# Output projections with their sums of squares accumulated on TensorE, and another order at the start of the up-projection

## The chip, the cores and the metric

The kernel runs on one core of one Trainium2 chip. The core has five engines with a queue each: TensorE (PE, matrix products; PEld is its weight load), VectorE (DVE), ScalarE (ACT), GpSimd (POOL) and SyncE (SP, which issues DMAs here). They run side by side and meet only through semaphores. The metric is the device time of one execution of the whole program in microseconds (us).

## The reference, cut to what matters

Two decoder layers over 1024 prompt and 32 sample tokens, width 1024. What the change touches is, in each layer, the output projection with its norm and residual, and the up-projection of the ConvFFN behind it:

```python
def rms_norm(x, g):
    y = xf * lax.rsqrt(jnp.mean(xf * xf, axis=-1, keepdims=True) + NORM_EPS)
    return (y * g.astype(jnp.float32)).astype(x.dtype)
...
    xp = xp + rms_norm(op, norm_mix_post[i])        # op: the mixer's output @ w_out
    hp = rms_norm(xp, norm_ffn_pre[i])
    fp, cp = conv_ffn(hp, ffn_w_up[i], ffn_conv_w[i], ffn_conv_b[i], ffn_w_down[i], ...)
...
def conv_ffn(h, w_up, conv_w, conv_b, w_down, prev):
    u = h @ w_up
    full = jnp.concatenate([prev.astype(u.dtype), u], axis=1)
    c = conv_b + sum(conv_w[j] * full[:, j:j + T] for j in range(CONV_W))
```

The sample tokens take the same path with their own conv state `prev`.

## The kernel before

Activations lie feature-major in SBUF as [128, 8, 1056] fp32: 8 blocks of 128 features (the keys k), 1056 tokens. The program is a row of stages, each with its own semaphores and an all-engine barrier at its end. Inside a stage the order on each engine is written out by hand; nothing reorders it.

**`stage_out`** (named "aout" in layer 0, "ro" in layer 1) multiplies by the 1024 x 1024 output weights in 12 steps, `STEPS`: 3 chunks c of 352 tokens (`CW`), and in each 4 steps q, every step making output blocks q and q + 4. A step is a Strassen-like scheme of 7 products of 4 matmuls of 176 columns (line L2044; a fp32 matmul stands as two rows in the trace), into banks a, d, b, c, a, cc, d. VectorE forms token mixes t1, t2, t4 (`mix_tokens`) and weight mixes (`mix_weights`), and empties the banks with five additions per step (L2238 to L2254, counted by `evac`); ScalarE copies bank a twice.

Then there are two norms for each chunk. The first: ScalarE squares each finished block (L2144), VectorE adds the squares up in `total` (L2190, `add_squares`, seven additions per chunk, the last ones one step late or, for the last chunk, behind the loop), TensorE sums over partitions with one matmul against ones (`sums`, L2054), ScalarE takes the root (L2107), VectorE the reciprocal (`invert`, L2194), and VectorE scales each key and adds the x of before, which SP fetched from DRAM (`residual`, L2207 and L2199). The second norm, over the new x, gives `K.rstd` for the up-projection: ScalarE squares the 8 keys (`square_again`, L2112) into the used-up source, VectorE folds 8 to 4 to 2 to 1 (`fold`, L2219), TensorE sums (`sums_again`, L2060), ScalarE root (L2116), VectorE reciprocal (`invert_again`, L2223). Chunk c's residual stands in chunk c + 1's steps 1 to 3; that of chunk 2 stands behind the loop. SP stores each finished chunk of x (`keep`, L2028), fetches the third chunk of the old x once chunk 0 is kept, and prefetches the first gate weights of the up-projection (`follow`, L2034).

**`Taps`** brings the conv taps and the conv state (16 rows of 5632) in and turns them on TensorE behind step 1 (L1914, L1916: 44 transposes of 16 x 128), VectorE copies them out of PSUM (L1921, L1922).

**`stage_ffn_up`** first norms x into `hT` on VectorE: for each key two pieces of 512 columns (`scale_half`, L2430) and one of the 32 samples (L2435), the lower four keys first. Then VectorE makes four token mixes of [128, 2112] (t1 L2462, t3 L2467, t2 L2470, t4 L2473) with the four weight mixes s1 to s4 (L2442 to L2449) between them. After that a loop over 22 pairs of blocks runs with 7 products of 8 matmuls each of 264 columns (L2369, order a, d, b, c, a, c, d). The gates of the first products are these lines:

```python
                    pe.wait_ge(first_done, j + 1)          # L2378, first product "a"
                    pe.wait_ge(scaled, 3 * HK)
...
                    pe.wait_ge(evac, ev(j, 0))             # L2383, product "d"; ev(0, 0) is 1
...
            act.wait_ge(zeroed, 2)                         # L2401
            act.sem_inc(first_done, 1)
...
                dve.wait_ge(tmade, 3)                      # L2472, ahead of t4
            dve.tensor_tensor(t4, b21, t2, ALU.subtract).then_inc(tmade, 1)
            for u in range(2):
                dve.memset(ubuf[u][:, 0:2], 0.0).then_inc(zeroed, 1)
            dve.sem_inc(conved, 1)
            dve.sem_inc(evac, 1)                           # L2477
```

## Time and profile before

| | us |
|---|---|
| median of 3 runs | 4861.34 |
| lowest, highest | 4851.31, 4864.03 |
| the profiled execution, its device time | 4863.29 |
| its span in the trace | 4861.7 |
| TensorE busy | 4188.1 (86%) |
| VectorE busy | 2951.7 (61%) |
| ScalarE busy | 1111.3 (23%) |
| GpSimd busy | 318.2 (7%) |

Busy time is the sum over the span; a busy TensorE is a modelled one, since matmuls are pipelined. Its mean granted clock was 0.93 of full speed. The shares are averages over stages with different limits, so the argument rests on timelines of single stages: a timeline lists the instructions of an engine in order of time, merged where they are alike, each with its start and length, and in brackets the idle time ahead of it and what ended it. L-numbers are lines of the kernel, "q" behind an engine's name is its queue.

### The profile page before, as it was taken

The numbers are of one execution on the slowest core, as the hardware profiler recorded it, in microseconds if no ns is written. First come the engines' busy times: TensorE is split into PE (matmuls) and PEld (weight loads), VectorE is DVE, ScalarE is ACT, GpSimd is POOL, SyncE is SP. The second block draws the span as 40 slices with busy tenths as digits, with TensorE's granted clock in tenths as the row PEclk, the third lists the DMA queues.
The fourth block names the chain that finished last, engine by engine and source line by source line (L and its number), as shares of the span: only waits on it lengthen the run. The fifth ranks groups of instructions, "written<-read, shape, count | busy, mean of one in ns | idle before, by whom it ended". The sixth has DMA issues, their size and how long they took to land. (4 is left out here: it accounts for less than half of the span.)

```text
span 4861.7 us, 83795 instructions
## 1 busy us (share of the span) xinstructions
PE 4188.1 (86%) x33219; PEld 3210.0 (66%) x33248; DVE 2951.7 (61%) x4318; ACT 1111.3 (23%) x2118; POOL 318.2 (7%) x443
## 2 busy tenths in 40 slices
PE   7998889877777879999996999678887859999998
PEld 5565335444434768887994655377875758888897
DVE  3799665379942665556465122478885665555465
ACT  1200454344432212222110011132222112222100
POOL 0000000300045000000000000022220000000000
PEclk9999999899978889999997999799998779999999
DMA  3012000299976211111452231422213221111343
GB/s 102 22 35 60 9 1 1 59 320 353 366 230 169 69 47 43 43 43 47 131 147 73 71 112 66 156 63 55 64 38 155 63 72 43 43 40 38 99 143 119
DMA packets 553343, 463.37 MB, mean 95 GB/s; under 512 B 77346, under 2 KB 472138, under 8 KB 548827
## 3 DMA queue, kind: packets, MB, share of 16 engines
q1 hardware_dynamic: 522210, 409.36, 26.8%
q10 hardware_dynamic: 21088, 32.80, 2.0%
q0 software_dynamic: 9728, 16.80, 1.2%
q8 instruction: 222, 3.64, 0.3%
q14 instruction: 95, 0.77, 0.0%
HBM read 397.01 MB, written 61.71 MB: 94 GB/s over the span
## 5 line engine op out<-in xcount | busy, mean ns | idle before, releaser
L313 PE MATMUL proj_acc<-hT,oT 128*128 128x352 f32 x864 | 258.7, 463 | 6.2 <-SPq L287 6.2
L313 PEld LDWEIGHTS proj_acc<-hT,oT 128*128 128x128 f32 x864 | 165.6, 192 | 99.6 <-SPq L287 7.1
L517 DVE TENSOR_SCALAR_CACHE_REDUCE oT<-scores,proj_cand 128x384 bf16<-128x384 f32 (+1 forms) x186 | 164.4, 943 | 1.1
L2416 ACT ACTIVATE fup_c<-fup_c 128x1072 f32<-128x1072 f32 x44 | 48.3, 1098 | 504.6 <-DVEq L2486 504.6
L3424 POOL TENSOR_TENSOR scan_om<-scan_low,scan_level 128x512 f32<-128x512 f32 x80 | 133.1, 1675 | 391.8 <-PE scan_u L3506 294.7
L1227 DVE MAX8 sstick_best<-vtok 32x8 f32<-32x4100 f32 x32 | 141.1, 4408 | 0.0
L1230 DVE MATCH_REPLACE8 vtok<-sstick_best,vtok 32x4100 f32<-32x4100 f32 x32 | 140.8, 4400 | 0.0
L2640 PE MATMUL fdown_acc<-hidden,h 128*128 128x176 f32 x792 | 124.5, 316 | 9.3 <-SPq L2603 9.3
L2640 PE MATMUL fdown_acc<-hidden,oT 128*128 128x176 f32 x792 | 123.8, 315 | 9.4 <-SPq L2603 9.4
L1140 ACT ACTIVATE sstick_kT<-sstick_tp 128x512 f32<-128x512 f32 x248 | 128.3, 597 | 3.6 <-PE sstick_tp L1033 3.5
L2512 DVE TENSOR_TENSOR fup_u<-rstd,fup_acc_c 128x512 f32<-128x512 f32 x44 | 30.3, 689 | 162.3 <-PE fup_acc_c L2369 162.3
L2640 PEld LDWEIGHTS fdown_acc<-hidden,h 128*128 128x128 f32 x792 | 121.4, 193 | 9.7 <-SPq L2603 9.7
L2640 PEld LDWEIGHTS fdown_acc<-hidden,oT 128*128 128x128 f32 x792 | 120.7, 192 | 9.9 <-SPq L2603 9.9
L2485 DVE SCALAR_TENSOR_TENSOR fup_c<-fup_u,taps,fup_c 128x1072 f32<-128x1072 f32 x88 | 117.4, 1335 | 13.4 <-DVE fup_c L2484 5.9
L2484 DVE SCALAR_TENSOR_TENSOR fup_c<-fup_u,taps,fup_c 128x1072 f32<-128x1072 f32 x88 | 117.4, 1335 | 12.2 <-DVE fup_c L2483 4.7
L1804 DVE SCALAR_TENSOR_TENSOR mixed<-xx,vectors,h 128x352 f32<-128x352 f32 (+1 forms) x128 | 69.9, 625 | 68.2 <-PEq L95 68.2
L2369 PE MATMUL fup_acc_a<-oT,w_up_first 128*128 128x264 f32 x352 | 84.7, 395 | 27.6 <-ACTq L2402 27.6
L2369 PE MATMUL fup_acc_a<-h,w_up_first 128*128 128x264 f32 x352 | 83.5, 391 | 27.5 <-ACTq L2402 27.5
L2499 DVE TENSOR_TENSOR fup_u<-rstd,fup_acc_c 128x528 f32<-128x528 f32 x44 | 31.0, 705 | 124.8 <-PE fup_acc_c L2369 124.8
L2413 ACT ACTIVATE fup_u<-fup_acc_a 128x512 f32<-128x512 f32 x44 | 26.3, 599 | 351.8 <-PE fup_acc_a L2369 351.8
L3506 PE MATMUL scan_u<-scan_Tm,scan_om 64*64 64x64 f32 x2560 | 95.3, 233 | 12.4 <-DVE scan_TT L3836 6.4
L3506 PEld LDWEIGHTS scan_u<-scan_Tm,scan_om 64*64 64x64 f32 x2560 | 90.1, 148 | 17.3 <-issue 17.2
(736 smaller groups left out, 9891.8 us busy)
## 6 DMA issues: line engine op xcount, KB each, us to landing
fup_w<-in_ffn_w_up SPq DMA_DIRECT2D x66, 512.0 KB, 4.9
h<-in_ffn_w_down SPq DMA_DIRECT2D x48, 704.0 KB, 4.7
oT<-in_ffn_w_down SPq DMA_DIRECT2D x48, 704.0 KB, 4.7
scores<-in_cache_sb_k SPq DMA_DIRECT2D x128, 256.0 KB, 5.9
qb<-in_cache_sb_k SPq DMA_DIRECT2D x128, 256.0 KB, 6.1
qi<-in_cache_sb_v SPq DMA_DIRECT2D x128, 256.0 KB, 5.9
ka<-in_cache_sb_v SPq DMA_DIRECT2D x128, 256.0 KB, 6.1
w_up_first<-in_ffn_w_up SPq DMA_DIRECT2D x22, 512.0 KB, 3.9
```

The source lines that it names most:

```text
L313: last = pe.matmul(acc[u][0:m, c, 0:CW], w[u][:, k, 0:m], hT[:, k, c * CW:(c + 1) * CW], start=(k == 0), stop=(k == KD - 1))
L517: self.mark(dve.tensor_scalar(self.junk[:, at:at + (CHOOSING[t] + 1) * P], score, at_least, 0.0, ALU.is_ge, ALU.add, accum_out=self.count[ ...
L1140: act.activation(kT[:, p % 2, :, i % 4, (i // 4) * P:(i // 4 + 1) * P], tp[t % 3][:, :].rearrange("p (f n) -> p f n", f=HP), ACT.Copy).the ...
L1227: link(dve.max(best[:, :], score))
L1230: link(dve.match_replace(score, best[:, :], score, LOW))
L1804: dve.scalar_tensor_tensor(out=m[:, k, at], in0=xx[:, k, at], scalar=column[:, k:k + 1], in1=h[:, k, at], op0=ALU.mult, op1=ALU.add).then_ ...
L2369: last = pe.matmul(acc[n][:, g, 0:GW], weights[:, k, :], moving[:, k, g * GW:(g + 1) * GW], start=begin and k == 0, stop=k == HK - 1, skip ...
L2484: link(dve.scalar_tensor_tensor(out=c, in0=ubuf[u][:, 1:1 + CO], scalar=tap[1], in1=c, op0=ALU.mult, op1=ALU.add))
L2485: link(dve.scalar_tensor_tensor(out=c, in0=ubuf[u][:, 2:2 + CO], scalar=tap[2], in1=c, op0=ALU.mult, op1=ALU.add))
L2640: last = pe.matmul(bank[n], weights[:, k, :], moving[:, k, :], start=begin and k == 0, stop=k == DOWN_K - 1, skip_group_check=True)
L3424: pool.tensor_tensor(om[:, heads(g), :], low2[:, heads(g), 0, :], level[:, l, :].unsqueeze(1).to_broadcast(full), ALU.mult).then_inc(om_re ...
L3506: last = pe.matmul(spot(h, c, False), om[half(c), h, :], Tm[half(c), h, :], start=True, stop=True, skip_group_check=True)
```

## The change

Sizes are as before, and the same values are computed, except for the order of additions.

- `Taps`: the state comes in four DMAs as 64 rows of 1408 and is turned by 11 transposes of 64 x 128; two copies put it in place.
- `sums` (first norm) accumulates three matmuls in PSUM: `total` and the two squares of a chunk's last step, which VectorE adds no more (5 additions per chunk). It stands in the next chunk's step 0 instead of 1. `invert` and `residual` move one step ahead likewise.
- Second norm: squares go into the free `before` buffer. Chunk 0 keeps the fold, one step earlier than before; chunks 1 and 2 have none, TensorE accumulates their 8 squares (`sums_of_all`) behind the loop. `square_again`, `root_again` and `invert_again` move with them.
- Chunk 0 is normed in `stage_out` (`normed`) behind the last evacuation, into the place that the up-projection reads.
- SP fetches the third chunk of x after `summed_again` 1, and `follow` now also brings the first value weights.
- `stage_ffn_up`: the two memsets come first, then four keys with 160 columns (`scale_first`, the rest of the first half) and the samples; then the other pieces. The first product waits for 8 scalings instead of 12.
- Buffers only: `raw`, `Z` in the recurrence, and `s4` and `inverse` in the down-projection lie elsewhere.

```diff
     def allocate(self, s):
-        self.state_rows = s.sb("state_rows", [16, 2 * D_FF])
+        self.state_rows = s.sb("state_rows", [64, KF // 2 * P])
...
-        sp.dma_start(self.state_rows[:, :], self.state.rearrange("b w n -> (b w) n")).then_inc(self.loaded, 16)
+        wide = KF // 2 * P
+        for j in range(4):
+            sp.dma_start(self.state_rows[16 * j:16 * j + 16, :], self.state.rearrange("b w n -> (b w) n")[:, j * wide:(j + 1) * wide])\
+              .then_inc(self.loaded, 16)
...
-        for m in range(M):
-            last = pe.transpose(acc[:, m // KF, m % KF * 16:m % KF * 16 + 16], self.state_rows[:, m * P:(m + 1) * P], K.ident[0:16, 0:16])
+        for i in range(KF // 2):
+            last = pe.transpose(acc[:, i // 8, i % 8 * 64:i % 8 * 64 + 64], self.state_rows[:, i * P:(i + 1) * P], K.ident[0:64, 0:64])
...
         def squares(c):
-            return src[:, :, chunk(c)]
+            return before[:, c % 2]
...
             keep(0)
+            sp.wait_ge(summed_again, 1)
             sp.dma_start(before[:, 0], x_before_dram[:, :, chunk(2)]).then_inc(fetched, 16)
...
             def sums(c):
-                pe.wait_ge(totalled, 7 * (c + 1))
+                pe.wait_ge(totalled, 5 * (c + 1))
...
-                pe.matmul(spare[:, 0, 0:CW], K.ones[:, :], total[:, :], start=True, stop=True).then_inc(summed, 1)
...
+                pe.matmul(spare[:, 0, 0:CW], K.ones[:, :], total[:, :], start=True, stop=False)
+                for i in range(2):
+                    pe.wait_ge(squared, 8 * c + 7 + i)
+                    last = pe.matmul(spare[:, 0, 0:CW], K.ones[:, :], square[:, i, :], start=False, stop=i == 1)
+                last.then_inc(summed, 1)
...
+            def sums_of_all(c):
+                if c == 1:
+                    pe.wait_ge(rooted_again, 1)
+                for k in range(KD):
+                    pe.wait_ge(squared_again, KD * c + k + 1)
+                    last = pe.matmul(spare[:, c, 0:CW], K.ones[:, :], squares(c)[:, k, :], start=k == 0, stop=k == KD - 1)
+                last.then_inc(summed_again, 1)
...
-                if c >= 1 and q == 1:
+                if c >= 1 and q == 0:
                     sums(c - 1)
-                if c == 2 and q == 2:
-                    sums_again(0)
+                if c == 2 and q == 1:
+                    sums_folded(0)
...
-            sums_again(1)
             sums(NCH - 1)
-            sums_again(NCH - 1)
+            sums_of_all(1)
+            sums_of_all(2)
...
-                if c >= 1 and q == 1:
+                if c >= 1 and q == 0:
                     root(c - 1)
-                if c == 2 and q == 0:
-                    square_again(0)
-                if c == 2 and q == 2:
+                if c >= 1 and q == 3:
+                    square_again(c - 1)
+                if c == 2 and q == 1:
                     root_again(0)
...
+            def normed(ks):
+                for k in ks:
+                    if k == 0:
+                        dve.wait_ge(inverted_again, 1)
+                        dve.wait_ge(product, 7 * 8)
+                    for low, high, shift in normed_pieces(0):
+                        dve.scalar_tensor_tensor(out=src[:, k, low + shift:high + shift], in0=dst[:, k, low:high], scalar=K.gain[:, k:k + 1],
+                                                 in1=K.rstd[:, low:high], op0=ALU.mult, op1=ALU.mult)
...
-            invert_again(0)
-            add_squares(LAST)
-            fold(1)
+            normed(tuple(range(KD)))
             invert(NCH - 1)
             residual(NCH - 1, tuple(range(KD)))
             invert_again(1)
-            fold(NCH - 1)
             invert_again(NCH - 1)
...
-                    pe.wait_ge(scaled, 3 * HK)
+                    pe.wait_ge(scaled, 2 * HK)
                     multiply("a", gate[:, lower, :], b11, True)
...
+            def scale_first(k):
+                at, low = slice(CW, 2 * GP), CW + GS
...
+            for u in range(2):
+                dve.memset(ubuf[u][:, 0:2], 0.0).then_inc(zeroed, 1)
             for k in range(HK):
-                scale_half(k, 0)
+                scale_first(k)
                 scale_samples(k)
             for k in range(HK):
-                scale_half(k, 1)
+                scale_second(k)
+            dve.wait_ge(scaled, 3 * HK)
             for k in range(HK, KD):
-                scale_half(k, 0)
-                scale_half(k, 1)
+                scale_first(k)
                 scale_samples(k)
+                scale_second(k)
             dve.wait_ge(scaled, 3 * KD)
...
-            for u in range(2):
-                dve.memset(ubuf[u][:, 0:2], 0.0).then_inc(zeroed, 1)
             dve.sem_inc(conved, 1)
             dve.sem_inc(evac, 1)
...
     def follow(self):
-        return [(self.w_up[:, :, :], up_first(self.I.ffn_w_up[self.layer]))]
+        W = self.I.ffn_w_up[self.layer].rearrange("(k p) n -> p k n", p=P)
+        return [(self.w_up[:, :, :], W[:, :, 0:P]), (self.w_up_value[:, :, :], W[:, :, D_FF:D_FF + P])]
```

The code is written by hand in the order in which each engine runs it. VectorE at the end of aout, from the last evacuation to the residual of chunk 2, before:

```order
L2254 TENSOR_TENSOR h<-aout_u,aout_acc_d 128x176
L2207 SCALAR_TENSOR_TENSOR h<-h,aout_gcol,aout_inverse 128x352 x2
L2199 TENSOR_TENSOR h<-h,aout_before 128x352 x2
L2223 RECIPROCAL rstd<-rstd 128x352
L2190 TENSOR_TENSOR aout_total<-aout_total,aout_square 128x352 x2
L2219 TENSOR_TENSOR oT<-oT 128x4x352
L2219 TENSOR_TENSOR oT<-oT 128x2x352
L2219 TENSOR_TENSOR oT<-oT 128x352
L2194 RECIPROCAL aout_inverse<-aout_inverse 128x352
```

and with the change, where the pair L2239 stands eight times:

```order
L2283 TENSOR_TENSOR h<-aout_u,aout_acc_d 128x176
L2239 SCALAR_TENSOR_TENSOR oT<-h,gain,rstd 128x256
L2239 SCALAR_TENSOR_TENSOR oT<-h,gain,rstd 128x96
...
L2214 RECIPROCAL aout_inverse<-aout_inverse 128x352
L2227 SCALAR_TENSOR_TENSOR h<-h,aout_gcol,aout_inverse 128x352 x2
```

What stood between the last evacuation and the reciprocal of chunk 2 has gone into the steps ahead or to TensorE, and the norming of chunk 0 stands there. TensorE behind the last product of aout, before:

```order
L2044 MATMUL aout_acc_d<-oT,aout_mixes 128x176 x4
L2060 MATMUL aout_spare<-oT,ones 128x352
L2054 MATMUL aout_spare<-aout_total,ones 128x352
L2060 MATMUL aout_spare<-oT,ones 128x352
L92 UNCONDITIONAL_BRANCH
```

and with the change:

```order
L2062 MATMUL aout_acc_d<-oT,aout_mixes 128x176 x4
L2072 MATMUL aout_spare<-aout_total,ones 128x352
L2075 MATMUL aout_spare<-aout_square,ones 128x352 x2
L2087 MATMUL aout_spare<-aout_before,ones 128x352 x16
L92 UNCONDITIONAL_BRANCH
```

The sum of chunk 2 (L2072, L2075) no longer stands behind that of the new chunk 1. VectorE in the up-projection of layer 0, before:

```order
L2430 SCALAR_TENSOR_TENSOR oT<-h,gain,rstd 128x2x256
L2435 SCALAR_TENSOR_TENSOR oT<-h,gain,rstd 128x4x8
...
L2462 TENSOR_TENSOR h<-oT 128x2112
...
L2473 TENSOR_TENSOR h<-oT,h 128x2112
L2475 MEMSET fup_u 128x2 x2
L2528 UNCONDITIONAL_BRANCH
```

and with the change:

```order
L2482 MEMSET fup_u 128x2 x2
L2454 SCALAR_TENSOR_TENSOR oT<-h,gain,rstd 128x160
L2465 SCALAR_TENSOR_TENSOR oT<-h,gain,rstd 128x4x8
...
L2460 SCALAR_TENSOR_TENSOR oT<-h,gain,rstd 128x2x256 x4
...
L2506 TENSOR_TENSOR h<-oT,h 128x2112
L2559 UNCONDITIONAL_BRANCH
```

The memsets have moved from behind t4 (L2473, now L2506) to the front; the two increments of semaphores behind t4 have no row here and stand where they stood.

## Rows read from the trace of the kernel before

**Rows 1.** Busy time of each engine in two windows: us, busy us (instructions), PEclk, DMA share, GB/s

```profile
1677.00:1709.00 32.00, 4.27 (x7) 1.68 (x6) 25.74 (x33) 9.17 (x20) 0.00 (x0) 0.56 0.25 90
1709.00:1733.00 24.00, 0.00 (x0) 0.00 (x0) 22.87 (x31) 0.00 (x0) 0.00 (x0) 0.50 0.24 66
```

**Rows 2.** Timeline, TensorE: start us, us, engine line op, shapes, count [idle before <- releaser]

```profile
1733.32 6.46 PE L2369 MATMUL fup_acc_a<-oT,w_up_first 128*128 128x264 f32 x16 [27.62 <-ACTq L2402]
...
1743.18 3.72 PE L2369 MATMUL fup_acc_b<-h 128*128 128x264 f32 x16
...
3974.73 5.34 PE L2369 MATMUL fup_acc_a<-h,w_up_first 128*128 128x264 f32 x16 [27.50 <-ACTq L2402]
...
3983.46 3.72 PE L2369 MATMUL fup_acc_b<-oT 128*128 128x264 f32 x16
```

**Rows 3.** Timeline, TensorE, around the turn of the conv state, both layers

```profile
1583.91 0.44 PE L1914 MATMUL aout_spare<-ident,aout_tap_rows 44*128 44x44 f32 x4 [1.11 <-DMA aout_state_rows<-in_state_ffn_conv]
1584.29 4.34 PE L1916 MATMUL aout_spare<-ident,aout_state_rows 16*128 16x16 f32 x44
...
1592.68 1.36 PE L2044 MATMUL aout_acc_b<-aout_t,aout_mixes 128*128 128x176 f32 x8
...
3827.22 2.89 PE L1916 MATMUL ro_spare<-ident,ro_state_rows 16*128 16x16 f32 x44
...
3835.40 1.36 PE L2044 MATMUL ro_acc_c<-h,ro_w 128*128 128x176 f32 x8
```

**Rows 4.** Timeline, TensorE, first steps of chunk 2 in aout

```profile
1643.37 1.43 PE L2044 MATMUL aout_acc_d<-aout_t,aout_mixes 128*128 128x176 f32 x8 [0.33 <-DVE h L2254]
...
1651.80 0.76 PE L2054 MATMUL aout_spare<-aout_total,ones 128*128 128x352 f32 x2
1652.39 1.36 PE L2044 MATMUL aout_acc_d<-aout_t,aout_mixes 128*128 128x176 f32 x8
1653.59 1.36 PE L2044 MATMUL aout_acc_b<-aout_t,aout_mixes 128*128 128x176 f32 x8
```

**Rows 5.** Timeline, VectorE, first evacuation of the step after 1616

```profile
1620.46 0.34 DVE L2238 TENSOR_TENSOR aout_u<-aout_p,aout_acc_b 128x176 f32<-128x176 f32 x1 [3.89 <-PE aout_acc_b L2044]
```

**Rows 6.** Timeline, VectorE, from the last product of aout to its end

```profile
1677.05 0.34 DVE L2254 TENSOR_TENSOR h<-aout_u,aout_acc_d 128x176 f32<-128x176 f32 x1 [0.85 <-PE aout_acc_d L2044]
...
1688.94 2.35 DVE L2194 RECIPROCAL aout_inverse<-aout_inverse 128x352 f32<-128x352 f32 x1 [3.40 <-ACT aout_inverse L2107]
1691.33 1.08 DVE L2207 SCALAR_TENSOR_TENSOR h<-h,aout_gcol,aout_inverse 128x352 f32<-128x352 f32 x2
...
1698.78 2.36 DVE L2223 RECIPROCAL rstd<-rstd 128x352 f32<-128x352 f32 x1
...
1706.33 2.35 DVE L2223 RECIPROCAL rstd<-rstd 128x352 f32<-128x352 f32 x1 [2.22 <-ACT rstd L2116]
```

**Rows 7.** Timeline, ScalarE and TensorE, in the same stretch

```profile
1677.42 0.50 ACT L2144 ACTIVATE aout_square<-h 128x352 f32<-128x352 f32 x1 [0.64 <-DVE h L2254]
...
1698.48 0.93 ACT L2112 ACTIVATE oT<-h 128x352 f32<-128x352 f32 x2 [0.44 <-DVE h L2199]
...
1704.16 1.54 PE L2060 MATMUL aout_spare<-oT,ones 128*128 128x352 f32 x2 [15.84 <-DVE oT L2219]
```

**Rows 8.** Timeline, VectorE, at the start of the up-projection of layer 0

```profile
1710.06 0.75 DVE L2430 SCALAR_TENSOR_TENSOR oT<-h,gain,rstd 128x512 f32<-128x512 f32 x1 [1.38 <-PEq L95]
1710.73 0.24 DVE L2435 SCALAR_TENSOR_TENSOR oT<-h,gain,rstd 128x32 f32<-128x32 f32 x1
...
1722.08 2.36 DVE L2462 TENSOR_TENSOR h<-oT 128x2112 f32<-128x2112 f32 x1
...
1727.95 2.35 DVE L2470 TENSOR_TENSOR h<-oT 128x2112 f32<-128x2112 f32 x1
```

**Rows 9.** Line L2477: engine, operation, count, duration ns, first and last start us

```profile
L2477 DVEq EVENT_SEMAPHORE  x2: 21/21/21, 1730.5 to 3971.9; - x2
```

**Rows 10.** DMA issues in aout: count, KB each, median us to landing

```profile
aout_before<-x_save SPq DMA_DIRECT2D x3, 1408.0 KB, 11.4
```

More of the change, by code:

```diff
@@ L2002, in squares, with normed_pieces @@
         def squares(c):
-            return src[:, :, chunk(c)]
+            return before[:, c % 2]
+        def normed_pieces(c):
+            pieces = []
+            for g in range(SEQ // GP):
+                low, high = max(c * CW, g * GP), min((c + 1) * CW, (g + 1) * GP, SEQ)
+                if low < high:
+                    pieces.append((low, high, g * GS))
+            return pieces
         @block.sync
@@ L2287, with stage_ffn_up @@
 PRODUCTS = 7
[L2290 removed]
+def stage_ffn_up(nc, K, name, w_up, x, saved, hT, taps, stateT, last_u, hidden, firsts, follow):
     W = w_up.rearrange("(k p) n -> p k n", p=P)
```

100 lines of the change are left out of this document (48 added, 52 removed).

## The prediction

> **What bounds the kernel now.** I read the busy times in windows first, then the timelines of TensorE, VectorE and ScalarE around the places that the diff touches. It is one core, and every stage ends in a barrier, so a microsecond gone from the path of a stage is gone from the total. The diff touches an output projection and the up-projection behind it, and each exists twice: in layer 0 ("aout") and, 2241 us later, in layer 1 ("ro"). I cost layer 0 and double it where layer 1 reads alike.
>
> Inside the projections TensorE is the bound, its products follow each other. From the last product at 1677 to the first of the up-projection at 1733 it is VectorE. [rows 1]: in the first 32 us TensorE works 4.3 and VectorE 25.7; in the next 24 us TensorE does nothing and VectorE 22.9, and the granted clock (PEclk) is 0.50, the level of 1.2 GHz. So the questions are how long VectorE's chain is, and what TensorE waits for at its end. [rows 2] answers the second: 27.6 us of idle, ended by ScalarE's queue at L2402. That is `first_done`, which ScalarE gives only after the two memsets of L2475, and these stand behind t4, the last token mix.
>
> **Term 1: turning the conv state.** 44 transposes of 16 rows become 11 of 64. [rows 3]: from the start of the 44 to 1592.68 pass 8.39 us with two products in them; a product takes 1.19 at full clock ([rows 4], 1652.39 to 1653.59), so 6.0 us are the turn (4.3) and the low clock after it (1.7). In layer 1 it is 8.18 us with three products: 4.6. A 16-row transpose costs 0.066 to 0.099 there; I put a 64-row one at 0.12, between 0.07 and 0.2, so 1.3 us for the 11. In layer 1 I count the cold part as gone, since the small work lasts under 2 us: -3.3. In layer 0 the state rows are waited for already (1.1 us, [rows 3]), and they now come in four DMAs, three more issues in SP's queue: I leave half of the cold part and 0.3 us of wait: -3.6. Together **-6.9** (ends -3.5 and -8.6). The copy out of PSUM becomes two, where VectorE has room.
>
> **Term 2: sums within chunks 1 and 2.** `sums` becomes three matmuls of 352 columns and moves to the head of a chunk. One costs 0.59 us in the stream ([rows 4], 1651.80 to 1652.39). Two calls with two more each are +2.4. But there TensorE stands 0.33 us today until an evacuation by VectorE is done ([rows 4], 1643.37), and the three fill this: +1.7. The two squares that they read end some 0.9 us after that evacuation, about when product "a" and the first of the three are through; no new wait. Two layers: **+3.4** (ends +3 and +4.5).
>
> Residuals, inverses and the fold each move one step ahead. VectorE then has up to 4.4 us behind the last evacuation of a step (an inverse 2.4, two keys 2.0). Its next evacuation comes 3.9 us after it today ([rows 5]), so it is half a microsecond late. TensorE notices only before its seventh product, 7.2 us into the step; less the three evacuations ahead of that (1.1) and the last one (0.35), the cover is 5.7. Cost nothing; it would cost what it passed 5.7 by.
>
> **Term 3: from the last product to the end of the stage.** Today 31.6 us pass from the last evacuation (1677.05) to the end of the last reciprocal (1706.33 plus 2.35, [rows 6]). With the change the last evacuation is followed by the norming of chunk 0: 8 times a piece of 256 and one of 96 columns. in [rows 8] 512 columns take 0.67 us to the next start, and 24 pieces, 16 of them long, 12.0, which leaves 0.16 for one of 32; between these lie 0.40 and 0.23, 8 times: 5.0, to 1682.4. Meanwhile the last square ends at 1677.9 ([rows 7]), the third sum at 1678.8, the root at 1679.4: hidden. A reciprocal of 2.4 ends at 1684.8. Eight keys of residual take 7.45 (1691.33 to 1698.78): 1692.2. Inverse 1 lasts until 1694.5. Beside it, behind the last add: a square (0.6 later, as 1699.41 to 1698.78 today, [rows 7]), the last matmul, a root of 0.55; then a reciprocal of 2.35. The matmul takes 0.76 at full clock ([rows 4]) and 1.54 at the low one ([rows 7]), so the end is 1696.9 or 1697.5. Gone are the add of squares, both folds and the waits of 3.40 and 2.22 ([rows 6]); late next is the residual itself. 31.6 less 20.1 is -11.5, two layers **-23.0** (ends -24 and -18). The 16 sums of chunks 1 and 2 run while TensorE would stand: 8 end near 1683.4, and 8 follow one key each, every 0.93 us.
>
> **Term 4: the start of the up-projection.** Eight pieces of 512 columns become 160, by the same line 0.30 instead of 0.67: 2.9 less. The memsets and one drain cost 0.2, so t1 starts 9.3 us after VectorE's start instead of 12.0 ([rows 8]). Product "a" needs the memsets and 8 short scalings and starts near +2.1. It gains less than that. Product "d" behind it waits for `evac`, which VectorE raises at L2477, behind t4, in both kernels. [rows 9]: it ran at 1730.5, 0.2 us after t2 ended (1727.95 plus 2.35) and 2.7 before t4 did: when t4's wait for t2 was over. With the chain 2.7 shorter that is +17.7, and "d" starts there. It starts cold: "a" has ended by +8.4, and TensorE idles nine microseconds. Today the cold product is "a": "a" and "d" take 9.9 us in layer 0 and 8.7 in layer 1 ([rows 2]), and with 3.6 for a warm "d" that leaves 6.3 and 5.2. If "d" costs the same, "b" starts at +24.0 (+23.0); today "a" and "d" are through at +33.1 (1743.18) and +32.0 (3983.46). t2, s2 and the copied bank are there by then. -9.0, two layers **-18.0** (ends -16 and -20). The loop behind it is TensorE's, and the gain stays.
>
> The value weights move into the prefetch of the stage before; today they come beside the scalings, and VectorE's 22.9 busy us of 24 leave no wait for them ([rows 1]), so nothing is gained. SP's queue: the fetch of the third chunk of x now waits for the sum of the first (near 1653.6, before 1646.6), with the weight loads and two stores behind it. It is needed at 1684.8 and takes 11.4 us ([rows 10]).
>
> **The sum** stands against the profiled execution, 4863.3 us (span 4861.7): -6.9 + 3.4 - 23.0 - 18.0 = -44.5, so 4818.8. The median of the three runs, 4861.3, is 2 us lower, and the runs reach from 4851 to 4864. I say **4818**.
>
> **A rule against a row.** L2477 ran only when t4's wait was over [rows 9]. The Trainium skill ("Perfetto Trace Analysis", the section on the DVE / Act engine instruction in the per-instruction lifecycle) has the sequencer free for the next instruction once one is pushed into the wait queue, before its semaphores are satisfied. By that rule L2477 would have run while t2 was still working; the trace says otherwise. What it would make of the time is rival 2.
>
> **Rivals.**
> 1. The clock in the tail. TensorE's clock falls after 1683 and stays low through the 8 sums of chunk 2. At 1.2 us each against a key every 0.93 they end near 1696.5, the root at 1697.2, the reciprocal at 1699.6: 2.6 us later, 5.2 for both layers, 4823. For it: TensorE stands 3.5 us ahead of them, and a window at this place was at 0.56 ([rows 1]). Against: they follow nearly back to back, and the cold products of [rows 2] (7.1 at 1.2 GHz all through) were faster before they ended. Chance 0.15.
> 2. `evac` is raised early. Without memsets between, the increments stand directly behind t4. If they run while t4 waits, "d" starts when s1 is ready, at +12.3, and "b" at +18.6: 5.4 us earlier, 10.8 for both, 4807. For it only that the queue holds two instructions less. Chance 0.08.
> 3. The cover is too thin: the 4.4 us grow past 5.7, and six steps per layer lose one microsecond each. 12 us back, 4830. For it: 1.3 us of slack; against: all its parts were measured among the same products. Chance 0.06.
> 4. Slower: the fetch of the third chunk is late, and the residual of chunk 2 waits. It costs from a landing 31 us after issue, and decides from 53, where it has eaten 22 us per layer; at 60 us the kernel takes 4877. The row says 11.4. Chance 0.01.
> 5. It doesn't do what it says: "a" stays behind the token mixes, and the norming is not covered. Then terms 1 and 2 and a few microseconds of the chain are left, 4855. Against: the memsets are now VectorE's first instructions. Chance 0.03.
>
> **How the numbers follow.** The forecast has the remaining 0.67. The ends of the terms reach from -49 to -33, so 4812 to 4828, and the spread of runs adds to both sides. The range of 4804 to 4830 takes in rivals 1 and 2. A measurement can tell about 0.3%, 14.6 us, from no change. Faster by more: 0.96; within: 0.03; slower: 0.01.
>
> **What would show it.** Right: TensorE's "a" starts 2 us after VectorE's start of the up-projection and "d" 15.6 us after "a", with some nine microseconds of idle ended by VectorE's queue, and "d" is the slow product; the last reciprocal of the output projection ends 20 us after the last evacuation. Wrong: "d" at s1 (rival 2); VectorE's last wait for ScalarE over 2 us (rival 1); idle rows of TensorE within steps (rival 3); a residual released by a DMA (rival 4). A total above 4835 would mean a missing term, most likely within term 2.

## The result, and the profile after

| | before | after |
|---|---|---|
| median of the runs, us | 4862.7 (4 runs) | 4816.1 (4 runs, 4807.6 to 4818.4) |
| the profiled execution, its device time | 4863.3 | 4818.4 |
| its span | 4861.7 | 4816.8 |

The ratio is 0.9905, with a 95% interval of 0.9893 to 0.9917: 46 us less (40 to 52). The profiled executions differ by 44.9. The forecast was 4818 with a range of 4804 to 4830, and -44.5.

The same four places as before, now in the trace of after. First the turn of the conv state; TensorE, both layers (start us, us, engine line op, shapes, count). It answers [rows 3].

```profile
1582.46 1.36 PE L2062 MATMUL aout_acc_d<-oT,aout_mixes 128*128 128x176 f32 x8
1583.75 0.44 PE L1917 MATMUL aout_spare<-ident,aout_tap_rows 44*128 44x44 f32 x4
1584.02 0.87 PE L1919 MATMUL aout_spare<-ident,aout_state_rows 64*128 64x64 f32 x11
1584.82 1.46 PE L2062 MATMUL aout_acc_a<-oT,aout_w 128*128 128x176 f32 x8
...
1587.32 1.36 PE L2062 MATMUL aout_acc_b<-aout_t,aout_mixes 128*128 128x176 f32 x8
...
3803.13 0.88 PE L1919 MATMUL ro_spare<-ident,ro_state_rows 64*128 64x64 f32 x11
```

No idle ahead of the tap rows, 0.80 us for the 11 transposes, and full-speed products behind them. From the last "d" ahead of the turn to "b" behind it pass 4.86 us. In layer 1 the same piece, to product "c", is 6.05 (3801.57 to 3807.62). Before, the two pieces began with these rows:

```profile
1581.45 1.36 PE L2044 MATMUL aout_acc_d<-oT,aout_mixes 128*128 128x176 f32 x8
3825.55 1.36 PE L2044 MATMUL ro_acc_d<-h,ro_mixes 128*128 128x176 f32 x8
```

and were 11.23 (to the 1592.68 of [rows 3]) and 9.85 (to 3835.40).

Then the sums at the head of chunk 1, TensorE:

```profile
1601.74 1.36 PE L2062 MATMUL aout_acc_a<-oT,aout_w 128*128 128x176 f32 x8
1602.93 0.76 PE L2072 MATMUL aout_spare<-aout_total,ones 128*128 128x352 f32 x2
1603.67 1.45 PE L2075 MATMUL aout_spare<-aout_square,ones 128*128 128x352 f32 x4
1604.96 1.36 PE L2062 MATMUL aout_acc_d<-aout_t,aout_mixes 128*128 128x176 f32 x8
```

"d" follows "a" by 3.22 us instead of 1.19, and the idle 0.33 of [rows 4] has gone into it. From the "a" of this step to the last evacuation pass 71.67 us in both layers; in before 69.94 and 69.95, in layer 0 from this row to the 1677.05 of [rows 6]:

```profile
1607.11 1.36 PE L2044 MATMUL aout_acc_a<-oT,aout_w 128*128 128x176 f32 x8
```

Then the tail, by which I mean the time from the last evacuation to the end of the last reciprocal; VectorE, and below it TensorE. It answers [rows 6, 7].

```profile
1673.41 0.34 DVE L2283 TENSOR_TENSOR h<-aout_u,aout_acc_d 128x176 f32<-128x176 f32 x1 [0.86 <-PE aout_acc_d L2062]
1673.67 5.08 DVE L2239 SCALAR_TENSOR_TENSOR oT<-h,gain,rstd 128x256 f32<-128x256 f32 x16
1678.67 2.35 DVE L2214 RECIPROCAL aout_inverse<-aout_inverse 128x352 f32<-128x352 f32 x1
...
1688.52 4.65 DVE L2252 RECIPROCAL rstd<-rstd 128x352 f32<-128x352 f32 x2
...
3892.52 0.34 DVE L2283 TENSOR_TENSOR oT<-ro_u,ro_acc_d 128x176 f32<-128x176 f32 x1 [0.86 <-PE ro_acc_d L2062]
...
3910.93 2.35 DVE L2252 RECIPROCAL rstd<-rstd 128x352 f32<-128x352 f32 x1 [0.97 <-ACT rstd L2144]
```

```profile
1675.03 4.90 PE L2087 MATMUL aout_spare<-aout_before,ones 128*128 128x352 f32 x16
1683.15 7.04 PE L2087 MATMUL aout_spare<-aout_before,ones 128*128 128x352 f32 x16 [3.22 <-ACT aout_before L2140]
...
3902.25 8.06 PE L2087 MATMUL ro_spare<-ro_before,ones 128*128 128x352 f32 x16 [3.22 <-ACT ro_before L2140]
```

In layer 0 VectorE waits for nothing between the last evacuation and 1693.17: 19.8 us, before 31.6. In layer 1 it is 20.8, since the last reciprocal waits 0.97 for ScalarE's root, which waits for the sums of chunk 2; these last 8.06 us instead of 7.04. The granted clock is 0.65 in a window within them (window, length, busy us of TensorE, its weight loads, VectorE, ScalarE, GpSimd, then PEclk, DMA share, GB/s):

```profile
3905.00:3910.00 5.00, 5.00 (x12) 2.82 (x11) 4.96 (x7) 1.92 (x4) 0.00 (x0) 0.65 0.21 76
```

Last, the start of the up-projection: VectorE's start and mixes, TensorE's first products, and line L2508, which is L2477 of before. It answers [rows 2, 8, 9].

```profile
1694.58 0.06 DVE L2482 MEMSET fup_u<- 128x2 f32 x1 [1.42 <-PEq L95]
...
1703.83 2.36 DVE L2495 TENSOR_TENSOR h<-oT 128x2112 f32<-128x2112 f32 x1
...
1709.70 2.35 DVE L2503 TENSOR_TENSOR h<-oT 128x2112 f32<-128x2112 f32 x1
```

```profile
1696.68 5.45 PE L2394 MATMUL fup_acc_a<-oT,w_up_both 128*128 128x264 f32 x16 [6.49 <-DVE oT L2465]
1712.27 6.20 PE L2394 MATMUL fup_acc_d<-h 128*128 128x264 f32 x16 [10.14 <-DVEq L2508]
1718.30 3.72 PE L2394 MATMUL fup_acc_b<-h 128*128 128x264 f32 x16
...
3932.26 5.54 PE L2394 MATMUL fup_acc_d<-oT 128*128 128x264 f32 x16 [9.10 <-DVEq L2508]
3937.64 3.72 PE L2394 MATMUL fup_acc_b<-oT 128*128 128x264 f32 x16
```

```profile
L2508 DVEq EVENT_SEMAPHORE  x2: 21/21/21, 1712.2 to 3932.2; - x2
```

Counted from VectorE's start (1694.58 and 3914.57), "a" starts at +2.1, "d" at +17.7, "b" at +23.7 and +23.1. Before, "b" came at +33.1 and +32.0. The idle of 27.6 ahead of "a" has become 6.5 ahead of "a" and 10.1 ahead of "d".

### The profile page after: what moved, and what is told of

It reads as the page before. It is cut to its first block and busy times, and to the rows that moved or that the text cites. A ratio compares the mean times of both kernels' runs of the same rounds, so it can differ in the third digit from the quotient of the medians.

```text
span 4816.8 us, 83854 instructions
## 1 busy us (share of the span) xinstructions
PE 4212.5 (87%) x33262; PEld 3222.6 (67%) x33262; DVE 2938.8 (61%) x4328; ACT 1112.3 (23%) x2118; POOL 319.1 (7%) x443
## 5 line engine op out<-in xcount | busy, mean ns | idle before, releaser
L2515 DVE SCALAR_TENSOR_TENSOR fup_c<-fup_u,taps,fup_c 128x1072 f32<-128x1072 f32 x88 | 117.5, 1335 | 12.2 <-DVE fup_c L2514 5.2
L1033 PE MATMUL sstick_tp<-ident,scores 128*128 128x128 f32 x512 | 76.7, 311 | 23.5 <-ACT sstick_kT L1140 23.5
L602 PE MATMUL stick_z<-stick_softplus,tri 128*128 128x512 f32 (+3 forms) x192 | 76.7, 523 | 23.4 <-DVE stick_softplus L706 23.2
```

The source lines that it names most:

```text
L602: last = pe.matmul(z[m % R][:, par, c:512], K.tri[:, :], soft[:, m % R, par, c:512], start=False, stop=True, skip_group_check=True)
L1033: last = pe.transpose(tp[t % 3][:, f * P:(f + 1) * P], kring(t % KR)[:, f * P:(f + 1) * P], K.ident[:, :])
L2515: link(dve.scalar_tensor_tensor(out=c, in0=ubuf[u][:, 1:1 + CO], scalar=tap[1], in1=c, op0=ALU.mult, op1=ALU.add))
```

## The experiments

The kernels of one group ran on one chip, beside the kernel before. Where a run is set against the kernel after, that is put at 0.9905 of before on the same chip, 4812.9 in the first group and 4812.6 in the second; in the third it ran itself. A ratio is good to about 0.0015, 7 us, so pieces of the timeline carry most of what follows, and the totals bound it.

**What "d" waits for.** Two kernels move the increments behind t4, one to the front, one ahead of t4 by a single instruction.

```diff
             for u in range(2):
                 dve.memset(ubuf[u][:, 0:2], 0.0).then_inc(zeroed, 1)
+            dve.sem_inc(conved, 1)
+            dve.sem_inc(evac, 1)
...
             dve.tensor_tensor(t4, b21, t2, ALU.subtract).then_inc(tmade, 1)
-            dve.sem_inc(conved, 1)
-            dve.sem_inc(evac, 1)
```

> The changed kernel, with the two increments of conved and evac at the front of VectorE's work in the up-projection, behind the memsets, instead of behind t4. Theory (product d waited for evac alone, and evac came only when t4's wait for t2 was over): d starts when s1 is ready, 12.2 us after VectorE's start instead of 17.7, still cold (6 us), and b at 18.3 instead of 23.7 (t2 is ready at 17.5). 5.4 us per layer, 10.8 in all: 4805 against 4816. Rival (d was held by s1, t1 or the copy of bank a, or the gain is given back in the loop): within 2 us of 4816.

Measured: 4803.1 us, ratio 0.9881 (0.9865 to 0.9898), 10 us below after. TensorE in layer 0, with VectorE's start at 1696.52:

```profile
1698.81 5.56 PE L2394 MATMUL fup_acc_a<-oT,w_up_both 128*128 128x264 f32 x16 [6.68 <-DVE oT L2465]
1709.05 5.51 PE L2394 MATMUL fup_acc_d<-h 128*128 128x264 f32 x16 [4.68 <-DVE h L2472]
1714.40 3.73 PE L2394 MATMUL fup_acc_b<-h 128*128 128x264 f32 x16
```

"d" starts at +12.5, released by its own operand s1 (L2472), and "b" at +17.9 in both layers: 5.8 and 5.2 earlier than in after. So the increment alone held "d", for 5 us a layer; the pieces give 11.0 in all, the total 10.

```diff
             mix_weights(0, 2, 0)
-            dve.wait_ge(tmade, 3)
-            dve.tensor_tensor(t4, b21, t2, ALU.subtract).then_inc(tmade, 1)
             dve.sem_inc(conved, 1)
             dve.sem_inc(evac, 1)
+            dve.wait_ge(tmade, 3)
+            dve.tensor_tensor(t4, b21, t2, ALU.subtract).then_inc(tmade, 1)
```

> The changed kernel, with the two increments moved by one instruction: ahead of t4 and its wait for t2, behind s3. Theory (an instruction whose semaphore is not yet there holds the queue, and what stands behind it, until it is): the increments now depend on t2's own wait, which is over when t3 is done. They run near +14.6 us after VectorE's start instead of +17.6, d starts with them, b at 20.6 instead of 23.7: 3.1 us less per layer. Rival (the queue runs ahead of waits, and the time of the increments came from the number of instructions ahead of them): one place less moves them by one instruction, under 0.7 us.

Measured: one run, 4808.1 us. The increment (here L2506) and the mixes around it, in layer 0, where VectorE's start is 1692.68; t3 is L2500, t2 L2503:

```profile
L2506 DVEq EVENT_SEMAPHORE  x2: 21/21/21, 1707.4 to 3922.0; - x2
```

```profile
1704.92 2.36 DVE L2500 TENSOR_TENSOR oT<-oT 128x2112 f32<-128x2112 f32 x1
...
1707.80 2.35 DVE L2503 TENSOR_TENSOR h<-oT 128x2112 f32<-128x2112 f32 x1
```

With t4 behind it the increment runs at +14.7, 0.1 us after t3 (L2500) has ended, and ahead of t2's work (1707.80). With t4 ahead of it (after) it runs 0.1 us after t2 has ended, at +17.6. Each time it comes when the wait of the last mix ahead of it is over, and never earlier: an instruction with an open wait held VectorE's queue. "d" started with the increment, at +14.8 in both layers, and "b" at +20.6 and +20.9, where +20.6 was expected.

**The memsets.** One kernel puts them back behind t4 in after, one puts them first in before and changes nothing else.

```diff
-            for u in range(2):
-                dve.memset(ubuf[u][:, 0:2], 0.0).then_inc(zeroed, 1)
             for k in range(HK):
...
             dve.tensor_tensor(t4, b21, t2, ALU.subtract).then_inc(tmade, 1)
+            for u in range(2):
+                dve.memset(ubuf[u][:, 0:2], 0.0).then_inc(zeroed, 1)
             dve.sem_inc(conved, 1)
```

> The changed kernel, with the two memsets behind t4 again. Theory (they gate the first product through ScalarE): a starts when t4 is done, +20.4 us after VectorE's start instead of +2.1, cold, 5.5 to 6.5 us, then d warm, 3.6: b at +29.9 instead of +23.7. 6.2 us per layer, 12.4 in all: 4828.5. Rival (the first product was held by the number of scalings that it waits for, 12 instead of 8): a few tenths, 4816.

Measured: 4823.6 us, ratio 0.9926 (0.9909 to 0.9942), 10.7 above after. TensorE in layer 0, with VectorE's start at 1693.03:

```profile
1713.49 5.68 PE L2394 MATMUL fup_acc_a<-oT,w_up_both 128*128 128x264 f32 x16 [24.82 <-ACTq L2427]
...
1722.57 2.61 PE L2394 MATMUL fup_acc_b<-h 128*128 128x264 f32 x11
```

The wait of [rows 2] is back, and "b" comes at +29.5, and at +29.7 in layer 1: 5.8 and 6.6 later.

```diff
+            for u in range(2):
+                dve.memset(ubuf[u][:, 0:2], 0.0).then_inc(zeroed, 1)
             for k in range(HK):
                 scale_half(k, 0)
...
-            for u in range(2):
-                dve.memset(ubuf[u][:, 0:2], 0.0).then_inc(zeroed, 1)
             dve.sem_inc(conved, 1)
```

> The kernel before with one edit: the two memsets stand first in VectorE's queue of the up-projection. Scalings, norms, turn and sums are those of before. Product 'a' then waits for its 12 scalings and starts near +9 instead of +23.6; 'd' still waits for the increment behind t4, which runs when t2 is over, 20.4 us after VectorE's start (1730.5 in the profile of before, VectorE's start there 1710.06). 'd' is then the slow product with 6.3 us, so 'b' comes at about +26.7 where before has +33.1: 6.4 a layer, 12.9 in all, and 5.4 of term 4's 18.3 belong to the shorter scalings (2.7 each). If instead 'a' early brings nothing since 'd' alone decides, the gain would be the same; if the memsets are not what 'a' waited for, it is 0.

Measured: 4849.5 us, ratio 0.9982 (0.9973 to 0.9991), 9 us below before (4 to 13). "b" at +26.8 (expected +26.7) and +27.0, where before has +33.1 and +32.0: 11.4 in all. "a" started at +6.2, not +9, since it waits for the scalings of the lower four keys only; that changes nothing behind it. Term 4 thus falls into 11 to 12 us for the memsets and 6 to 7 for the shorter scalings.

**Norming chunk 0 inside.** The call of `normed` is dropped, and the up-projection scales whole pieces of 512 columns again.

```diff
-            normed(tuple(range(KD)))
             invert(NCH - 1)
...
-                at, low = slice(CW, 2 * GP), CW + GS
+                at = slice(0, 2 * GP)
...
```

> The changed kernel without the norming of chunk 0 inside the output projection; the up-projection norms it, with pieces of 512 columns instead of 160, all else alike. Theory (of the 5.0 us of norming inside, only the 2.2 lie in the cover of square, sum and root): the output projection gets 2.8 us shorter, the up-projection 2.9 longer, sum 0 within 1: 4816. Rival (norming inside is hidden work, which is what makes the change fast): the up-projection's 2.9 us come on top, 5.8 for two layers: 4822.

Measured: 4811.2 us, ratio 0.9898 (0.9881 to 0.9914), the same as after within the spread. VectorE in layer 0:

```profile
1669.27 0.34 DVE L2283 TENSOR_TENSOR h<-aout_u,aout_acc_d 128x176 f32<-128x176 f32 x1 [0.86 <-PE aout_acc_d L2062]
1671.67 2.35 DVE L2214 RECIPROCAL aout_inverse<-aout_inverse 128x352 f32<-128x352 f32 x1 [2.07 <-ACT aout_inverse L2135]
1681.52 4.66 DVE L2252 RECIPROCAL rstd<-rstd 128x352 f32<-128x352 f32 x2
```

The reciprocal of chunk 2 waits 2.07 us for the root, and the tail is 16.9 us instead of 19.8. The start of the up-projection gives it back: t1 starts at +12.2 instead of +9.25, "b" at +26.1 instead of +23.7. Five microseconds of VectorE's work moved from one side of the barrier to the other and hid two of waiting, but as two pieces a key (256 and 96 columns) they cost 5.0 there, where the longer scalings cost 2.9 here.

**The turn of the conv state.** Term 1 was the one with a wrong size, so four kernels went to it and to the spread.

> The kernel after, word for word, once more beside the others. It says how far a second measurement of one and the same kernel lies from the first (ratio to before 0.9905), and it is the kernel that the other three of this group are set against, so that no value has to be carried over from another chip. Both theories expect 0.990, within 0.0015; the pieces of the timeline (4.9 us around the turn, 19.8 of tail, 23.7 to 'b' in layer 0) should come back within 0.1 to 0.3 us, since nothing in them waits for a transfer.

Measured: 4814.5 us (4803.7 to 4819.5), ratio 0.9906 (0.9893 to 0.9920). The turn is again 4.86 us in layer 0. The tail is 20.1 and 19.8, "b" at +23.0 and +23.6: the last reciprocal waited 0.30 in layer 0 this time and not at all in layer 1, and the cold "d" took 5.45 and 6.12. So "b" came back within 0.7, not within the 0.3 expected, and pieces with a cold product in them are good to that. The profiled execution took 4803.7 us, 11 under the median and 14.7 under the one of after, and 8.7 of that it had gained before the tail of aout (last evacuation at 1664.74). That is the spread with which totals have to be read.

```diff
-        self.state_rows = s.sb("state_rows", [64, KF // 2 * P])
+        self.state_rows = s.sb("state_rows", [16, 2 * D_FF])
...
-        for i in range(KF // 2):
-            last = pe.transpose(acc[:, i // 8, i % 8 * 64:i % 8 * 64 + 64], self.state_rows[:, i * P:(i + 1) * P], K.ident[0:64, 0:64])
+        for m in range(M):
+            last = pe.transpose(acc[:, m // KF, m % KF * 16:m % KF * 16 + 16], self.state_rows[:, m * P:(m + 1) * P], K.ident[0:16, 0:16])
...
```

> The kernel after with the turning of the conv state as before: one DMA of 16 rows, 44 transposes of 16 rows. It undoes term 1 alone. By the two timelines the turn gave back 6.4 us in layer 0 (11.23 to 4.86 from the end of step 1 to 'b' of step 2) and about 3.7 in layer 1, so the theory as measured expects +10.1 us against the kernel after; the prediction's term 1 says +6.9. By the ratio of after to before (0.9905) the kernel after would stand at 4812.9 on a chip whose before is 4859; the difference is to be read in the timeline too: the 44 transposes take 4.3 and 2.9 us, the two products behind them go at the low clock, and a wait of about a microsecond for the state's DMA comes back in layer 0. If the wait for the DMA was an accident of one execution, it is missing here and the difference is 9.0.

Measured: 4817.3 us, ratio 0.9918 (0.9904 to 0.9931), 4.7 above after. TensorE:

```profile
1583.54 1.36 PE L2056 MATMUL aout_acc_d<-oT,aout_mixes 128*128 128x176 f32 x8
1585.67 0.44 PE L1914 MATMUL aout_spare<-ident,aout_tap_rows 44*128 44x44 f32 x4 [0.78 <-DMA aout_state_rows<-in_state_ffn_conv]
1586.05 3.99 PE L1916 MATMUL aout_spare<-ident,aout_state_rows 16*128 16x16 f32 x44
...
1594.51 1.36 PE L2056 MATMUL aout_acc_b<-aout_t,aout_mixes 128*128 128x176 f32 x8
```

The piece is 10.97 us, and 9.84 in layer 1: 6.1 and 3.8 more than in after, 9.9 in all, as expected. The total shows half of it and leaves room for the rest (the two ratios differ by 0.0013, and each interval reaches 0.0013 to both sides). So the opposite kernel was run, before with the new turn alone; its diff is this one read backwards, on before.

> The kernel before with one edit: the conv state comes as 64 rows in four DMAs and is turned by 11 transposes. By the timelines of before and after that alone gives 6.4 us in layer 0 and 3.8 in layer 1, -10.2 against before; by the prediction's sizes -6.9. The rival is that part of it is given back: the total of the kernel with the old turn was only 4.4 us above the kernel after, where the places that the edit touches read 9.9. If that is more than spread, this run shows 4 to 5 us too, and a later row of the timeline shows a new wait; if it was spread, the total comes out between -7 and -13 and no row behind the turn waits longer than in before.

Measured: 4849.0 us, ratio 0.9973 (0.9964 to 0.9983) over ten runs: 13 us below before, 8 to 17.5 (the medians differ by 10). The piece in layer 0 is 4.86 us (1583.26 to 1588.12), with no wait and no slow product, and the one in layer 1 is 6.04. The interval holds the 10.2 of the timelines and not the 6.9 of the prediction. TensorE's longest waits behind the turn are those of before (27.6 and 15.8 us), and the tail is 31.6 us again. So the rival, that part is given back, has nothing for it here.

Part of why it is more than predicted, the last kernel of this group tells: the 11 transposes issued four times over.

```diff
-        for i in range(KF // 2):
+        for i in [n for _ in range(4) for n in range(KF // 2)]:
```

> The kernel after with the 11 transposes issued four times over into the same place: 44 transposes as before, but of 64 rows. The prediction put one at 0.12 us; the trace of after has 11 in 0.80, 0.073 each. By 0.073 the 33 extra ones cost 2.4 us a layer, by 0.12 4.0. Open is the granted clock behind them: if it is the length of the small work that lets the clock fall (44 transposes of 16 rows before: 4.3 and 2.9 us, then slow products), products behind these 44 are slow too and cost another 1.7 in layer 0: +4.8 + 1.7 to 3.4 in all. If it is the few rows in use that let it fall, the products stay at 1.19 us each and the sum is +4.8.

Measured: 4809.9 us (4803.9 to 4817.7), no difference from after in the total, where +4.8 was expected; the pieces give +4.1. TensorE in layer 1, and the granted clock of the two stretches:

```profile
3800.70 2.91 PE L1919 MATMUL ro_spare<-ident,ro_state_rows 64*128 64x64 f32 x44
3803.54 1.46 PE L2062 MATMUL ro_acc_a<-h,ro_w 128*128 128x176 f32 x8
```

```profile
3800.43:3803.54 3.11, 3.11 (x50) 3.04 (x49) 2.90 (x5) 0.50 (x1) 0.00 (x0) 1.00 1.06 375
3803.54:3806.00 2.46, 2.46 (x18) 2.46 (x17) 0.11 (x1) 0.32 (x1) 0.00 (x0) 1.00 0.51 172
```

and the same place in the kernel with the old turn (44 transposes of 16 rows):

```profile
3806.52 2.90 PE L1916 MATMUL ro_spare<-ident,ro_state_rows 16*128 16x16 f32 x44
3809.35 2.67 PE L2056 MATMUL ro_acc_a<-h,ro_w 128*128 128x176 f32 x8
```

```profile
3806.15:3809.35 3.20, 3.20 (x49) 3.12 (x49) 2.99 (x5) 0.50 (x1) 0.00 (x0) 1.00 1.06 367
3809.35:3811.81 2.46, 2.46 (x11) 2.46 (x9) 0.03 (x1) 0.00 (x0) 0.00 (x0) 0.52 0.75 255
```

44 transposes take the same 2.9 us whether they have 16 rows or 64. Behind the ones of 16 rows the granted clock was 0.52, the level of 1.2 GHz, and the next product took twice its time; behind those of 64 it stayed at 1.00. The 33 extra ones cost 2.05 us a layer (the piece is 6.91 and 8.08), 0.062 each. The expectation put the question as one of rows; but with the rows the second operand goes from 16 x 16 to 64 x 64, so the run doesn't say which of the two made the difference. The length of the small work didn't: it was 2.9 us both times.

**The cover of VectorE's steps.** An extra reciprocal (2.35 us, its result unused) in the first step of chunks 1 and 2.

```diff
...
                     residual(c - 1, (0, 1))
+                    dve.reciprocal(idle[:, :], inverse[:, :])
```

> The kernel after with one extra reciprocal of 352 columns (2.35 us, its result is not used) in VectorE's queue in the first step of chunks 1 and 2, behind the real inverse and the first two keys of the residual: four steps in all over both layers. It tests the cover. The prediction says that VectorE may be 5.7 us long behind the last evacuation of a step before TensorE stands; the parts are 4.4 now, 6.8 with the extra one. By the prediction this costs 1.1 us in each of four steps, 4.4 us, with an idle row of TensorE of about a microsecond in each. If the cover is larger than 6.8, it costs nothing; if it is already used up in the kernel after, the full 2.35 shows up each time, 9.4.

Measured: 4812.7 us, ratio 0.9906 (0.9891 to 0.9922), no difference in the total, where +4.4 was expected; the four waits come to 2.6. TensorE in the steps behind, chunk 1 and chunk 2:

```profile
1619.78 1.46 PE L2063 MATMUL aout_acc_d<-oT,aout_mixes 128*128 128x176 f32 x8 [0.79 <-DVE h L2274]
...
1656.27 1.46 PE L2063 MATMUL aout_acc_d<-oT,aout_mixes 128*128 128x176 f32 x8 [0.20 <-DVE h L2274]
```

The seventh product, as the prediction had it, is the one that waits. It is late by 0.95 us in chunk 1 and by 0.36 in chunk 2, where a sum of 0.59 stands ahead in TensorE's queue; the same two waits are in layer 1. The extra work ran 6.8 us against a cover of 5.7; less the 0.95 that is a cover of 5.8. In after both steps have no such row.

**The fold of chunk 2.** In after its eight squares are added by TensorE; here VectorE folds them again.

```diff
             sums_of_all(1)
-            sums_of_all(2)
+            pe.wait_ge(folded, 6)
+            pe.matmul(spare[:, 2, 0:CW], K.ones[:, :], squares(2)[:, 0, :], start=True, stop=True).then_inc(summed_again, 1)
...
             invert_again(1)
+            fold(NCH - 1)
             invert_again(NCH - 1)
```

> The kernel after with the second norm of chunk 2 as before: VectorE folds the eight squares 8 to 4 to 2 to 1 and TensorE sums once. It undoes one of the parts of term 3, that of the last chunk alone. Behind the last add the chain is then a square (0.5), three folds (3.05 in sum by the line of the folds), one matmul (1.54 at the low clock), a root and a reciprocal, where now the inverse of chunk 1 (2.35) covers square, matmul and root. VectorE's inverse of chunk 1 may stand ahead of the folds, so it is the folds and then an open wait of about 2.2 that come back: +5.2 us in layer 0 and +4.4 in layer 1, 9.6 in all, and the tail is 25 us instead of 19.8. The rival: the residual and its squares already set the end, and the folds slip in beside them; then it costs only the 3.05 of the folds a layer, 6.1.

Measured: 4819.3 us, ratio 0.9914 (0.9899 to 0.9930), 4.8 above after on the same chip. VectorE in layer 0, last evacuation at 1667.84:

```profile
1682.94 2.35 DVE L2254 RECIPROCAL rstd<-rstd 128x352 f32<-128x352 f32 x1
1685.20 3.05 DVE L2250 TENSOR_TENSOR aout_before<-aout_before 128x1408 f32<-128x1408 f32 x3
1690.47 2.35 DVE L2254 RECIPROCAL rstd<-rstd 128x352 f32<-128x352 f32 x1 [2.22 <-ACT rstd L2145]
```

The folds stand behind the inverse of chunk 1 and the wait of 2.22 is open, as in [rows 6]. The tail is 25.0 us in both layers, 5.2 more than the 19.8 of layer 0 of after and 4.2 more than its 20.8 in layer 1. It does not slip in beside anything. The total moved by half of these 9.4 us, and the two intervals (0.9899 to 0.9930, 0.9893 to 0.9920) overlap, so this rests on the rows. Elsewhere too: over the seven kernels whose pieces moved by 9 us or more the ratios add up to some 68 us and the pieces to 76. Each ratio agrees with its pieces within its interval, but the totals can't exclude that a small part is given back elsewhere.

**Both edits that leave the queue freer.** The increment first, and chunk 0 normed in the up-projection:

> Both edits tried one by one before, together on the kernel after: the increment that 'd' waits for stands first, and chunk 0 is normed at the start of the up-projection as before the change. If norming inside the output projection is worth nothing, as its single run said (tail 2.85 us shorter, start of the up-projection 2.9 longer), this kernel equals the one with the early increment alone, 0.988 of before (4802 here), and its tail reads 16.9 us and 'b' comes 2.9 later than +17.9, at +20.8. The rival: with 'd' behind its own operand alone the start of the up-projection is TensorE's, and the longer scalings cost less than they save, 'b' at +19.5 and the total 2 to 3 us lower.

Measured: 4802.1 us (4795.1 to 4804.9), ratio 0.9876 (0.9860 to 0.9892). The tail is 16.9 us, "d" starts at +15.5 and "b" at +20.7 in layer 0 (+21.1 in layer 1), so the two halves of the trade cancel once more. This kernel and the one with the increment alone (0.9881) can't be told apart; both beat after, by 10 and 12 us in their medians.

## Why the prediction was right, point by point

| term | predicted | in the two timelines |
|---|---|---|
| 1 turn | -6.9 (-3.6, -3.3) | -10.2 (-6.4, -3.8) |
| 2 sums in the chunks | +3.4 | +3.4 (+1.7, +1.7) |
| 3 tail | -23.0 | -22.7 (-11.9, -10.9) |
| 4 start of the up-projection | -18.0 (-9.1, -9.0) | -18.3 (-9.4, -8.9) |
| sum | -44.5 | -47.8; profiled executions -44.9 |

The four terms overshoot the profiled difference by 2.9 us. That lies outside the terms: from "b" of the first up-projection to the start of ro pass 2.0 us more than in before, steps 0 and 1 of aout start 0.5 us earlier and take 1.5 more, the same stretch of ro takes 1.1 less, and 0.9 more pass behind the second "b". No run was made for these; executions of one kernel differ by more. So the total of 4818 fitted closer than its parts deserve: that the 3.3 us missing in term 1 met 2.9 us that no term had is luck.

**Term 1 is mis-sized by 3.3 us**, nearly all in layer 0. The step said "I leave half of the cold part and 0.3 us of wait". Neither was there: the 1.11 of wait in [rows 3] went with the 0.3 that I had added (1.4), and the cold half did (0.85). A 64-row transpose cost 0.073 instead of the 0.12 chosen, 0.5 a layer. The sum, 0.5 + 0.5 + 0.85 + 1.4, is the 3.3.

The wait was misread. One DMA of 352 KB was waited for until 7.0 us after its issue, in before and again with the old turn; where it happened to be issued 7.9 us ahead, in the kernel with the memsets alone, it wasn't waited for. The four DMAs take up to 3.5 us to issue, and still after and the ten other kernels with them show no wait in layer 0, even where the turn began 3.0 us behind the end of the last issue (the kernel without the inner norming) or 5.6 behind the start of the first (the one with the extra reciprocal). I had counted the three issues more as a loss. But only part of the 1.11 is thereby shown to be the four DMAs' doing: in six of these eleven profiles the turn began over 7.0 us behind the start of the first issue, in after 7.6, where the one DMA would have been there as well. The other five (5.6 to 6.7) are those that show the four to be sooner. The reason for the cold half was wrong too: "the small work lasts under 2 us", with nothing said of what the work is. With the transposes four times over it lasts 2.9 us, and the granted clock stays at 1.00. In the three kernels with 16-row transposes the products behind were slow in both layers, with and without a wait ahead.

**Term 2** is right to a tenth, the 0.33 of idle that pays for part of it included. The first square is ready 0.15 us late for the second matmul: 1603.67, where 1602.93 and the 0.59 of a sum give 1603.52.

**Term 3** is right in each row: the norming takes 5.0 us to the next start (predicted 5.0), the residual 7.47 (from 1681.05; predicted 7.45), and the last reciprocal follows the one ahead of it at once. Rival 1, the low clock in the sums of chunk 2, is there in part: of sixteen tails in the eight profiles that share it, eleven had the last reciprocal directly behind the one ahead of it, and five had it wait, 0.30, 0.72, 0.83, 0.93 and 0.97 us, never the 2.6 of the rival. In before TensorE's last sum was on the path (1.54 us between the folds and the root, [rows 7]); with the change the sums are off it in most of these tails and never more than a microsecond late. Of the 22.7 us the kernel with the fold of chunk 2 tests 9.4, and norming inside is worth nothing; the other 13, the fold of chunk 1, the squares and the wait of 3.40, are read from the rows, and no kernel put them back.

**Term 4**: "a" at +2.1, "d" at +17.7 and "b" at +23.7 against +2.1, +17.7 and +24.0 (layer 1: +23.1 against +23.0). Its one doubtful step was when the increment behind t4 would run, and it rested on a single row, [rows 9]. Two experiments moved that increment, and both times it ran where the row said. The Trainium skill ("Perfetto Trace Analysis", the section on the DVE / Act engine instruction in the per-instruction lifecycle) lets the sequencer go on as soon as an instruction is in the wait queue. By that the increment would not have cared whether t4 stood ahead of it; it moved from +17.6 to +14.7. So rival 2 was wrong as a mechanism, and right in its price: with the increment truly early "b" came 11.0 us sooner over both layers (10 in the total), where the rival had 10.8.

Rival 3 fell with the cover measured at 5.8 us against 4.4 in use, rival 4 with the fetch, which landed 7.2 and 9.7 us (medians) after issue and ended no wait. Rival 5 fell at the first row of the up-projection.

What was argued and not measured: that the value weights in the prefetch bring nothing. No kernel undid that part alone. The trace of before points the same way: its three weight fetches there are issued within 2.1 us of VectorE's start and fetches of this tile (`fup_w`) land 4.9 us after issue (median), while the first weight mix of after starts at +11.5.

## What to carry to other kernels

Count an increment of a semaphore as standing behind every wait ahead of it in its queue, even if the work behind that wait is none of its business; the row of that instruction in the trace says when it ran, and the cheapest edit here was to put it first. Before moving work across a barrier, cost it on the side where it lands: the norming cost five where it landed, saved three where it had been and hid two of waiting, so it was worth nothing, while shortening the chain itself (no folds, memsets first) was worth all of its price. And when a small transposition stands between products, use more rows for it: it was fewer instructions here, and the products behind it kept their clock.

## What the runs showed of the hardware that I had not expected

- 44 transposes took 2.9 us with 16 and with 64 rows (2.90 and 2.91), at a granted clock of 1.00. Behind 16 rows it then fell in both layers of all three kernels that had them (0.50 to 0.66 in the windows right behind), and the next products took up to 2.5 us from start to start where 1.19 is full speed; in layer 0 of before and of the kernel with the old turn it was low already within the transposes (4.34 and 3.99 us at 0.59 and 0.66), behind the wait for the state; behind 64 rows it stayed at 1.00 (windows of after and of the kernel with 44 of them).
- An instruction of VectorE with an open wait held back the semaphore instruction behind it: 1712.2 with t4 ahead, when t2 had ended at 1712.05, and with t4 behind it 0.1 us after the end of t3.
- Four DMAs of 88 KB into 64 partitions were all there at the latest 5.6 us after the start of the first issue in one profile, and 3.0 us after the end of the last issue in another; one of 352 KB into 16 partitions was waited for until 7.0 us after the start of its issue, in two profiles.
